# Mixture-of-experts stage of a two-layer diffusion trunk: the expert's hidden rows turned by sixteen VectorE transposes instead of two TensorE transposes and a ScalarE copy

## The reference

```python
def moe_ffn(tok, router_w, router_bias, w_gate, w_up, w_down, s_gate, s_up, s_down):
    ...
    def body(y, b):
        rows = lax.dynamic_slice_in_dim(tok_buf, b * MOE_BLOCK, MOE_BLOCK)   # 128 token numbers
        wb = lax.dynamic_slice_in_dim(w_buf, b * MOE_BLOCK, MOE_BLOCK)
        e = block_e[b]
        xb = x_pad[rows]
        hb = jax.nn.silu(xb @ w_gate[e]) * (xb @ w_up[e])                    # 128 x 256
        return y.at[rows].add((hb @ w_down[e]) * wb[:, None]), None
    ...
```

## Time and profile before

| | |
|---|---|
| median of 3 runs | 2861.16 us (2856.9 to 2862.29) |
| the profiled execution's own time | 2862.66 us |
| its span | 2860.8 us |
| mean granted TensorE clock | 0.976 |
| PE, DVE, ACT, POOL busy | 94%, 65%, 47%, 18% of the span |

### The profile page before, as it was taken

How to read it: one execution, slowest core, us unless ns; L and a number is a source line. 1 busy time by engine, 2 the same in 40 slices (tenths; PEclk the granted TensorE clock), 3 DMA queues, 4 the chain that set the end, 5 groups by cost and what they waited for, 6 DMA issues and landing times. The chain is left out here.

```text
span 2860.8 us, 40299 instructions
## 1 busy us (share of the span) xinstructions
PE 2691.1 (94%) x14086; PEld 1224.5 (43%) x14087; DVE 1847.5 (65%) x3359; ACT 1350.4 (47%) x3130; POOL 506.4 (18%) x404
## 2 busy tenths in 40 slices
PE   7998999899899999999999698997999999999994
PEld 2444666445333433434434274443333334333332
DVE  4995555566667666666765545666676766666655
ACT  1113555201166666666665340012656666666653
POOL 0000000111022222222222211100222222222212
PEclk9999999999999999999999899998999999999997
DMA  9777300201499999999999622016999999999996
GB/s 356 269 266 214 125 16 8 80 30 45 170 358 349 334 317 349 357 355 344 378 335 309 225 89 87 30 44 238 330 322 329 306 373 358 349 379 294 330 342 206
DMA packets 147092, 714.98 MB, mean 250 GB/s; under 512 B 16702, under 2 KB 22078, under 8 KB 94665
## 3 DMA queue, kind: packets, MB, share of 16 engines
q1 hardware_dynamic: 104252, 556.14, 49.8%
q0 software_dynamic: 42336, 154.16, 21.1%
q10 hardware_dynamic: 304, 2.11, 0.2%
HBM read 597.50 MB, written 114.84 MB: 249 GB/s over the span
## 5 line engine op out<-in xcount | busy, mean ns | idle before, releaser
L1671 ACT ACTIVATE xT<-xt_blocks 32x256 f32<-32x256 f32 x2208 | 913.8, 414 | 43.1 <-DVE xt_blocks L1538 15.6
L1750 PE MATMUL exG<-ring,xT 128*32 128x512 f32 (+2 forms) x2352 | 701.3, 598 | 4.7 <-DMA ring<-in_exp_w_up_dram 4.2
L1750 PEld LDWEIGHTS exG<-ring,xT 128*32 128x32 f32 (+2 forms) x2352 | 232.1, 140 | 311.3 <-issue 306.2
L1784 PE MATMUL exD<-ring,ex_hT 128*32 128x512 f32 (+2 forms) x1176 | 355.9, 605 | 2.4 <-DVE w_o L1576 1.2
L1543 DVE TENSOR_SCALAR ex_e<-ex_e 128x256 f32<-128x256 f32 x142 | 43.3, 305 | 431.0 <-ACT ex_e L1683 403.5
L1544 DVE RECIPROCAL ex_e<-ex_e 128x256 f32<-128x256 f32 x142 | 249.0, 1753 | 4.9
L1683 ACT ACTIVATE ex_e<-exG 128x256 f32<-128x256 f32 x142 | 54.5, 384 | 315.0 <-PE exG L1750 315.0
L1750 PE MATMUL exG<-oT,xT 128*32 128x512 f32 (+2 forms) x592 | 197.7, 599 | 1.3 <-DVE xT L1532 1.3
L1750 PE MATMUL exG<-w_fnet,xT 128*32 128x512 f32 (+2 forms) x608 | 176.9, 600 | 2.3 <-issue 2.3
L1502 DVE TENSOR_TENSOR mod<-place,slots 128x1024 bf16<-128x1024 f32 (+3 forms) x196 | 174.2, 913 | 5.6 <-PEq L234 4.7
L1478 POOL DMA_INDIRECT y_scratch<-w_fnet,idx_out x72 | 120.7, 1677 | 294.3 <-DMA y_scratch<-w_fnet,idx_out 238.4
(11 more groups left out here) (422 smaller groups left out, 4328.2 us busy)
## 6 DMA issues: line engine op xcount, KB each, us to landing
ring<-in_exp_w_gate_dram SPq DMA_DIRECT2D x64, 1024.0 KB
ring<-in_exp_w_up_dram SPq DMA_DIRECT2D x64, 1024.0 KB
ring<-in_exp_w_down_dram SPq DMA_DIRECT2D x64, 1024.0 KB
ada_w<-in_w_ada_dram SPq DMA_DIRECT2D x48, 512.0 KB, 5.5
oT<-in_exp_w_gate_dram SPq DMA_DIRECT2D x17, 1024.0 KB
oT<-in_exp_w_up_dram SPq DMA_DIRECT2D x17, 1024.0 KB
oT<-in_exp_w_down_dram SPq DMA_DIRECT2D x17, 1024.0 KB
fT<-in_exp_w_gate_dram SPq DMA_DIRECT2D x17, 1024.0 KB
```

The lines of the kernel that those rows point to most:

```text
L1671: last = act.activation(xT[m * UNIT:(m + 1) * UNIT, par, :, a * UNIT:(a + 1) * UNIT], parts[a * UNIT:(a + 1) * UNIT, m], ACT.Copy)
L1750: last = pe.matmul(psG[par][p:p + m], xT[:, par, k, p:p + m], ring[s % RING][:, 0:2, k * FF:(k + 1) * FF], start=k == 0, stop=k == KT - 1)
L1784: last = pe.matmul(psD[p:p + m, c], hT[:, k * P + p:k * P + p + m], ring[s % RING][:, 2, k * D + c * 512:k * D + (c + 1) * 512], start=k = ...
```

## The change

`turn_hidden` on PE, `turned` on ACT, the bank `exH` and the semaphore `H_mm` go. In their place DVE runs `spread(b)` right behind `hidden(b)`: sixteen transposes, each of 32 partitions x 64 elements (2 x 32), from partition group a of `ex_h` to partition group m of `ex_hT`, so that all 16 pairs of groups are done. `ex_hT` becomes two buffers. `hidden` now waits for `hT_done` of two turns before in place of `H_mm`, and `spread` waits for `h_done` of its own turn and for `d_mm` of two turns before. `gate_up` is no longer split. The loop over blocks that did not fit changes in the same way.

```diff
-                hT = sb("ex_hT", [P, FF])
+                hT = sb("ex_hT", [P, 2, FF])
...
-                        def hidden(b, par, lag):
+                        def hidden(b, par):
...
-                            after(dve, H_mm, b, lag)
+                            at_least(dve, hT_done, b - 1)
...
+                        def spread(b, par, free):
+
+                            dve.wait_ge(h_done, b + 1)
+                            at_least(dve, d_mm, free)
+                            for a in range(Q):
+                                for m in range(Q):
+                                    last = dve.transpose(
+                                        hT[m * UNIT:(m + 1) * UNIT, par].rearrange("p (k t) -> p k t", k=FK)[:, :, a * UNIT:(a + 1) * UNIT],
+                                        hid[a * UNIT:(a + 1) * UNIT, par].rearrange("t (k p) -> t k p", k=FK)[:, :, m * UNIT:(m + 1) * UNIT])
+                            last.then_inc(hT_done, 1)
...
-                            hidden(b, par, 2)
+                            hidden(b, par)
+                            spread(b, par, b)
...
-                        def turned(b):
-                            act.wait_ge(H_mm, b + 1)
-                            act.wait_ge(d_mm, b + 1)
-                            act.activation(hT[:], psH[:, 0:FF], ACT.Copy).then_inc(hT_done, 1)
...
-                            turned(b - 1)
                             gates(b, b % 2)
...
-                        def turn_hidden(b, par):
-                            pe.wait_ge(h_done, b + 1)
-                            after(pe, hT_done, b, 1)
-                            for k in range(FK):
-                                last = pe.transpose(psH[:, k * P:(k + 1) * P], hid[:, par, k * P:(k + 1) * P], ident[:])
-                            last.then_inc(H_mm, 1)
...
-                            gate_up(b, par, range(SPLIT))
-                            turn_hidden(b - 1, 1 - par)
-                            gate_up(b, par, range(SPLIT, KT))
+                            gate_up(b, par)
...
                         with dve.Fori(0, blocks(dve)) as i:
                             onehot_over(T + 1 + i, i + 1, 1)
                             hidden_over(T + i, i)
+                            spread(T + i, GP, T + 1 + i)
...
-                        turn_hidden(T - 1, 1 - GP)
                         down(T - 1)
```

More of the change, by code:

```diff
@@ L1382, in experts @@
                 psD = ps("exD", [P, 2, 512])
-                psI, psH = ps("exI", [P, 512]), ps("exH", [P, 512])
+                psI = ps("exI", [P, 512])
                 hot_done, idx_own, idx_done = (own_sems[n] for n in ("hot_done", "idx_own", "idx_done"))
@@ L1387, in experts @@
                 blocks_done, moved = sem("xt_blocks_done"), sem("xT_moved")
-                H_mm, hT_done, d_mm, y_done, out_idx = (sem(n) for n in ("H_mm", "ex_hT_done", "ex_d_mm", "ex_y_done", "out_idx"))
+                hT_done, d_mm, y_done, out_idx = (sem(n) for n in ("ex_hT_done", "ex_d_mm", "ex_y_done", "out_idx"))
                 h_own, all_added = sem("ex_h_own"), sem("all_added")
@@ L1392, in experts @@
                     "caps_in", "ks_done", "gen_own", "ex_rows_done", "ex_rows_out", "table_in"))
-                HAND, AHEAD, SPLIT, Q = 2, 4, 5, P // UNIT
+                HAND, AHEAD, Q = 2, 4, P // UNIT
                 def rows_read(eng, b):
@@ L1557, in hidden_over @@
                             dve.wait_ge(g_mm, b + 1)
-                            dve.wait_ge(H_mm, b)
+                            dve.wait_ge(hT_done, b)
                             dve.tensor_tensor(hid[:, GP].rearrange("t (k p) -> t p k", k=FK),
@@ L1632, in _ @@
                         indices(4, 0, 2)
-                        hidden(0, 0, 2)
+                        hidden(0, 0)
+                        spread(0, 0, 0)
                         for b in range(1, T):
@@ L1700, in _ @@
                                 rows(T, T % 2, 2)
-                        turned(T - 1)
                         act.wait_ge(table_in, 16)
@@ L1706, in _ @@
                             act.activation(e[:], psG[GP][:, 0], ACT.Exp, scale=-1.0).then_inc(e_done, 1)
-                            turned(T + i)
                             rows(T + 1 + i, GP, 1)
@@ L1739, in turn_rows, with gate_up @@
                             last.then_inc(X_mm, 1)
[L1741 to L1748, removed]
+                        def gate_up(b, par):
+                            for s, _, _, _, _ in turns[b]:
+                                if first[s] == b:
+                                    pe.wait_ge(w_in[s % RING], 32 * (s // RING + 1))
+                            columns_ready(pe, b)
+                            after(pe, h_done, b, 2)
+                            for k in range(KT):
                                 for s, _, p, m in pieces(turns[b]):
@@ L1751, in gate_up @@
                                                      start=k == 0, stop=k == KT - 1)
-                            if some[-1] == KT - 1:
-                                last.then_inc(g_mm, 1)
+                            last.then_inc(g_mm, 1)
                         def gate_up_over(b, i):
@@ L1783, in down @@
                                     for s, _, p, m in pieces(turns[b]):
-                                        last = pe.matmul(psD[p:p + m, c], hT[:, k * P + p:k * P + p + m],
+                                        last = pe.matmul(psD[p:p + m, c], hT[:, b % 2, k * P + p:k * P + p + m],
                                                          ring[s % RING][:, 2, k * D + c * 512:k * D + (c + 1) * 512],
@@ L1794, in down_over @@
                                 for k in range(FK):
-                                    last = pe.matmul(psD[:, c], hT[:, k * P:(k + 1) * P],
+                                    last = pe.matmul(psD[:, c], hT[:, GP, k * P:(k + 1) * P],
                                                      ring[E % RING][:, 2, k * D + c * 512:k * D + (c + 1) * 512],
@@ L1805, in _ @@
                         index(2, 0)
-                        gate_up(0, 0, range(KT))
+                        gate_up(0, 0)
                         turn_rows(1, 1, 16)
@@ L1828, in _ @@
                             index_over(T + 1 + i, i + 1)
-                            turn_hidden(T + i, GP)
                             down_over(T + i, i)
```

## The result

The changed kernel takes 2996.03 us (median, 2995.25 to 2996.82, 4 runs) against 2859.43 us before (2856.9 to 2862.29): a ratio of 1.048, 95% interval 1.0466 to 1.0494. It is 4.8% slower. The forecast was 2996 us.

What follows compares the result with a forecast made beforehand. PE bounds the kernel before; DVE, at 12.10 us per turn, becomes the bound. Layer spans of +64.9 and +59.2 plus 10.2 at stage ends give +134 us on 2862.66, less 1.5 for the median: 2996 us, range 2910 to 3065.

Steps and rivals of the forecast that it cites:

- PE is the bound, DVE has about 3 us to spare: Experts stages before the change: PE busy all of 100 us, DVE 68, waiting about 3 us per turn.
- The step of 0.259 us: DVE's `spread`: each small transpose costs 0.247 us plus a 0.012 us gap, without overlap.
- The lower bound of 0.162: DVE's `spread`: the step if transposes overlap across partition groups, 0.247 - 0.085 us, or less.
- DVE's turn of 12.10 us: Steady turns: 7.76 us without idling plus 4.34 for `spread`, against PE's 10.8, so DVE becomes the bound.
- The span from turn 1 to 68, 816.5 us: Each layer: 66 turns of 12.10 us, one of 10.95, and 6.97 for `overflow()`.
- What PE and ACT save counts for nothing: Steady turns: PE's saving becomes a wait; ACT's removed 0.38 us copy counts for nothing.
- PE's 0.30 us: PE's turn: mean saving from removing its two transposes, 0.21 us with one expert and 0.45 with two.
- The stages' ends, 5.1 us per layer: Last turn and the block that did not fit: 6.8 us more per layer, 1.7 recovered, net 5.1.
- The sum, +134 us: Whole kernel: layer 0 +64.9 us, layer 1 +59.2, stage ends 10.2, in all +134.
- Rival 1: DVE's transposes overlap across partition groups; DVE turn 10.55 us, PE stays the bound, 2828 us; chance 0.12.
- Rival 2: Step near balance, or transfers don't follow a shorter turn: 2845 to 2875 us, about 2860; chance 0.06.
- Rival 3: PE's granted clock falls as it waits over 1 us each turn: 3020 to 3115 us, about 3060; chance 0.07.

Runs made afterwards that it cites:

- e2: Changed kernel, but each of the sixteen transposes stays within one partition group, the group changing only at every fourth: 2996.89 us (one run, layer 1 routed otherwise).
- e3: Changed kernel with sixteen transposes within their partition groups, ordered so the group changes at every one: 3140.64 us (one run, layer 1 routed otherwise).
- e8: Changed kernel with `spread(b)` moved behind `weigh(b - 1)` and the next turn's `onehot`: 2967.45 us, ratio 1.0386.
- e5: Kernel before, PE's transposes and ACT's copy kept, with sixteen small DVE transposes added into a tile nobody reads: 2988.0 us, ratio 1.045.
- e11: Changed kernel with one 128 x 256 DVE transpose in place of the sixteen, in layer 1 alone: 2920.03 us, ratio 1.0211.
- e4: Changed kernel with one 128 x 256 DVE transpose in place of the sixteen, in both layers: 2963.01 us, with extra blocks in layer 1.
- e10: Changed kernel with one wide DVE transpose into PSUM, then four blocks moved by DVE, twelve by ACT: 2852.15 us, ratio 0.9975 to the kernel before.

## Why the prediction was right, point by point

- **PE is the bound, DVE has about 3 us to spare:** right. Twelve transposes (3.2 us with the wait) nearly fit, sixteen (4.2) don't.
- **The step of 0.259 us:** measured 0.249. The duration was put at 0.247 and is 0.236, the gap at 0.012 and is 0.013. The choice to go by ACT's sixteen copies and not by DVE's overlap within one group is what made the forecast, and e2 and e3 show that it was for the right reason. The lower bound of 0.162 was itself too high for overlapping ones: 0.127 from end to end.
- **DVE's turn of 12.10 us:** measured 12.00; the step was 0.01 shorter, 0.16 us in sixteen, and turns with two experts have a little more in `onehot`; the 0.20 us for `hidden`'s end was right, as e8 shows.
- **The span from turn 1 to 68, 816.5 us:** measured 815.1 and 811.1. With the measured turn of 12.00 the sum gives 66 x 12.00 + 10.85 + 6.97 = 809.8. Layer 1 is close to that. Layer 0 comes near 816.5 only by a turn that the sum did not have: its second is 15.7 us long (exponentials at 792.94 and 808.68), with PE 3.60 us without work for the one-hot matrix and then at half the clock, as told below.
- **What PE and ACT save counts for nothing:** right, by e5. The working of PE's 0.30 us has a slip: the tenth product lies nine steps of 0.43 behind the first, at 1009.82 and not at 1009.92. Nothing hangs on it. Gate and up of a turn take 7.03 us with one expert and 7.07 with two, where they mostly took 7.25 and 7.58, a mean of 0.33 us less.
- **The stages' ends, 5.1 us per layer:** too small. In layer 0, from the exponential of turn 68 to ACT's copy of the last gathered rows was 1593.02 - 1546.94 = 46.1 us and is 1663.81 - 1608.07 = 55.7, so 9.7 more; in layer 1 it was 46.4 and is 56.4. The order of waits was as said; most of what the term had left out is the clock, below. For layer 0 the sum said 70.0 us and the rows give 1663.81 - 1593.02 = 70.8, because three things made up for most of the 4.6: the main span is 1.4 us shorter than forecast; from the exponential of turn 0 to that of turn 1 it is 10.47 us in place of 11.80, with no `turned(0)` and no PE transposes in between; and the stage began 1.1 us earlier in this execution. That last one is chance: the exponential of turn 0 stands at 782.47 here and at 786.26 in e11, which has the same layer 0. In layer 1 the main span is 5.4 us under the forecast and the end 4.9 over it.
- **The sum, +134 us:** measured 2996.03 - 2859.43 = +136.6. The forecast stood on a time before of 2861.16, so 1.7 us of the agreement come from there. That 2996 was met to the microsecond is luck; single terms are off by 1 to 5 us and cancel.
- **Rival 1, overlap across groups:** excluded. **Rival 2, transfers bound a shorter turn:** no matter here, where the turn got longer; the waits of e4 and e10 point to it, without proof. **Rival 3, the clock falls in steady turns:** it did not; with a wait of 1.2 us in each turn it stays at 1.00 in the window above.

## What to carry to other kernels

Before work is moved to an engine with idle time, take that engine's turn from a stretch where it never idles and compare it, with the new work, to the turn of the engine that is relieved; below the difference the work is nearly free, above it every microsecond is paid in full and the relief is worth nothing. Price a row of small independent instructions by the step between them, not by the elements, and look whether successive ones start on the same partitions. And an experiment that spoils an early layer's output can change how much work a later layer has: read it in the stage before that, or spoil only the last.

## What the runs showed of the hardware

Small DVE instructions that start on the same partitions as the one before overlap it: each adds 0.127 us at a duration near 0.2; if the input's or the output's group changes, the step is the whole duration and a gap, 0.249 us. Sixteen within their groups, in an order that changes the group at every one, take 3.98 us in place of 2.51. ACT has such a gap too: twelve copies of 32 x 64 in e10 took 2.70 us, 0.225 each, at a mean duration of 0.214.

TensorE's speed after a long wait. The timeline of PE in the kernel after, in the last turns of layer 0:

```profile
1638.70 5.94 PE L1781 MATMUL exD<-ring,ex_hT 128*32 128x512 f32 x32 [5.47 <-DVE w_o L1587]
...
1656.54 5.37 PE L1792 MATMUL exD<-oT,ex_hT 128*128 128x512 f32 x8 [4.63 <-issue]
```

After 5.47 us without work, `down` of the last turn took 5.94 us; the same 32 records took 3.64 before. After 4.63 us, the last block's took 5.37, where it was 3.67. The 2.3 and 1.7 us together are most of the 4.6 by which the stage's end was underestimated. The windows of the kernel after show the granted clock (the number before the last two) in the midst of these two `down` and between them:

```profile
1639.00:1643.00 4.00, 4.00 (x24) 0.96 (x20) 0.00 (x0) 0.00 (x0) 1.38 (x1) 0.50 0.58 66
1645.00:1656.00 11.00, 6.92 (x40) 5.93 (x38) 8.62 (x21) 0.38 (x1) 1.55 (x1) 1.00 0.29 48
1657.00:1660.00 3.00, 3.00 (x5) 1.35 (x4) 0.67 (x5) 0.00 (x0) 1.00 (x1) 0.50 0.00 0
```

0.50 is the lower of the two levels, 1.2 GHz in place of 2.4, and single records of the last block's `down` took up to 1.06 us, against 0.59 at full speed. In the kernel before, where PE had waited 1.25 us ahead of the same `down`, the window is at 1.00:

```profile
1574.00:1578.00 4.00, 3.71 (x33) 1.27 (x34) 0.22 (x3) 0.00 (x0) 1.55 (x1) 1.00 0.41 41
```

In the second turn of layer 0 the same is seen: after 3.60 us of waiting, `down` took 5.40 us, and the window 797.00 to 799.00 is at 0.50. A wait of 1.2 us in every turn had no such price: the clock stays at 1.00 in the steady window.
